# Three edits to a two-block network kernel: earlier split pieces in a narrow projection, a rotated key added once, chain products ahead of dense quarters

## The reference, cut to what matters

```python
# first network: output projection of the attention, a residual with a gate
h = h + gm * (jnp.concatenate([y_w, y_g, y_n], axis=-1) @ w_out[l])

# recurrent mix: inputs of its chunks, with decay products P
kk = kk / norm(kk);  k = k * (1 + (a - 1) * k_a)
bonus = sum(r * k * r_k) * v

# latent attention: one rotated key for all 8 heads
k_rope = _apply_rope(k_rope, cos, sin)
logits = (jnp.einsum('bhqd,bhkd->bhqk', q_nope, k_nope)
          + jnp.einsum('bhqd,bkd->bhqk', q_rope, k_rope))
```

## Time and profile before

| | |
|---|---|
| median of the runs | 2359.54 us |
| profiled execution, its own time | 2362.72 us |
| its span | 2361.4 us |
| mean granted TensorE clock | 0.984 |
| TensorE matmul busy | 2257.7 us, 96% |
| TensorE weight load busy | 1914.6 us, 81% |
| VectorE busy | 1501.5 us, 64% |
| ScalarE busy | 954.9 us, 40% |
| GpSimd busy | 367.7 us, 16% |

### The profile page before, as it was taken

How to read it: one execution, slowest core, us unless ns; L and a number is a source line. 1 busy time by engine, 2 the same in 40 slices (tenths; PEclk the granted TensorE clock), 3 DMA queues, 4 the chain that set the end, 5 groups by cost and what they waited for, 6 DMA issues and landing times. The chain is left out here.

```text
span 2361.4 us, 36947 instructions
## 1 busy us (share of the span) xinstructions
PE 2257.7 (96%) x14328; PEld 1914.6 (81%) x14328; DVE 1501.5 (64%) x2311; ACT 954.9 (40%) x1534; POOL 367.7 (16%) x365
## 2 busy tenths in 40 slices
PE   6999999999999999999999999979999999998998
PEld 4888887666678888878888876669998998898998
DVE  4666766565675666666565346556667766876874
ACT  4222223455442222242222244545446334555763
POOL 1000001000000000000000010039995476000000
PEclk9999999999999999999999999999999999999999
DMA  7554445111134444434443242124544232244544
GB/s 280 190 189 178 171 165 178 72 37 54 54 134 160 168 175 170 169 119 178 160 177 129 98 129 80 55 87 154 191 168 167 94 115 73 90 146 158 179 175 144
DMA packets 52615, 331.03 MB, mean 140 GB/s; under 512 B 6545, under 2 KB 7825, under 8 KB 21649
## 3 DMA queue, kind: packets, MB, share of 16 engines
q1 hardware_dynamic: 49040, 319.15, 37.4%
q0 software_dynamic: 3456, 10.25, 1.5%
HBM read 325.56 MB, written 3.80 MB: 139 GB/s over the span
## 5 line engine op out<-in xcount | busy, mean ns | idle before, releaser
L1183 PE MATMUL bank<-u_hi,whi 128*128 128x512 f32 (+1 forms) x2512 | 867.6, 345 | 32.5 <-DVE u_lo L1137 14.9
L1184 PE MATMUL bank<-u_lo,whi 128*128 128x512 f32 (+1 forms) x2512 | 848.7, 338 | 0.0
L1185 PE MATMUL bank<-u_hi,wlo 128*128 128x512 f32 (+1 forms) x2512 | 848.1, 338 | 0.0
L568 DVE TENSOR_TENSOR wlo<-raw,whi 128x2048 fp32r<-128x2048 f32 (+2 forms) x207 | 433.3, 2093 | 317.0 <-ACT whi L566 317.0
L1183 PEld LDWEIGHTS bank<-u_hi,whi 128*128 128x128 f32 x2512 | 477.2, 190 | 108.9 <-issue 29.5
L1185 PEld LDWEIGHTS bank<-u_hi,wlo 128*128 128x128 f32 x2512 | 477.5, 190 | 51.6
L1184 PEld LDWEIGHTS bank<-u_lo,whi 128*128 128x128 f32 x2512 | 477.8, 190 | 48.8 <-issue 0.2
L566 ACT ACTIVATE whi<-raw 128x2048 fp32r<-128x2048 f32 (+2 forms) x207 | 353.1, 1706 | 340.6 <-PE bank L1185 254.0
L1245 ACT ACTIVATE sil<-bank 128x512 f32<-128x512 f32 (+1 forms) x88 | 47.8, 544 | 541.7 <-PE bank L1185 541.7
L1183 PE MATMUL bank<-hidden_hi,whi 128*128 128x512 f32 x528 | 205.4, 389 | 0.0
L1184 PE MATMUL bank<-hidden_lo,whi 128*128 128x512 f32 x528 | 205.4, 389 | 0.0
(11 more groups left out here) (426 smaller groups left out, 2907.2 us busy)
## 6 DMA issues: line engine op xcount, KB each, us to landing
raw<-in_stream SPq DMA_DIRECT2D x231, 1024.0 KB, 4.8
raw<-in_stream SPq DMA_DIRECT2D x80, 704.0 KB, 4.0
first_ada<-in_stream SPq DMA_DIRECT2D x8, 1024.0 KB, 16.4
raw<-in_stream SPq DMA_DIRECT2D x8, 768.0 KB, 4.3
skew<-rpb_rows POOLq DMA_DIRECT2D x8, 336.0 KB, 6.2
nbr_bias<-skew POOLq DMA_DIRECT2D x24, 112.0 KB, 3.5
h<-in_tokens SPq DMA_DIRECT2D x1, 2048.0 KB, 11.5
uq_ukv<-in_small POOLq DMA_DIRECT2D x1, 1536.0 KB, 8.0
```

Source lines behind the costliest of these rows:

```text
L568: v.tensor_tensor(self.lo[to][:, 0:n], raw[:, 0:n], self.hi[to][:, 0:n].bitcast(F32), ALU.subtract).then_inc(self.s_lo, 1)
L1183: pe.q.matmul(dst, w[0], x[0], start=start, stop=False)
L1184: pe.q.matmul(dst, w[0], x[1], start=False, stop=False)
L1185: return pe.q.matmul(dst, w[1], x[0], start=False, stop=stop)
```

## The change

It makes three edits. In the narrow projection a tile emits two pieces of the split instead of one (the wide one stays). The rotated key is added into head 0 alone by VectorE, and ScalarE copies it to the 7 others; the scores of the latent attention wait for the copy. In the recurrent mix the three quarters of `dense(3)` are emitted behind the chain instead of ahead of it, together with the four that stood there.

```diff
--- before.py
+++ after.py
@@ -1655,6 +1655,8 @@
                         split_begin(*((PHASE[("out", l)], i // 4 + 1) if i < 12 else (PHASE[("up2", l)], 0)))
                 if k % step == step - 1:
                     split_next()
+                    if qn != T:
+                        split_next()
                     yield step * (0.69 if qn == T else 0.36)
             done = (st.s_pe, g + 1) if i % 4 == 3 else tile_done
 
@@ -2229,7 +2231,6 @@
     bb = dve.do(dve.q.tensor_tensor(aa[:, :, :], kk[:, :, :], aa[:, :, :], ALU.mult))
     dve.after(bb, grown)
     beta = dve.do(dve.q.tensor_tensor(aa[:, :, :], aa[:, :, :], dec[:, :, :], ALU.mult))
-    dense(3)
     dve.after(kp, faded, *[mixed[c] for c in range(4)])
     for c in range(4):
         t = dve.do(dve.q.scalar_tensor_tensor(out=bonus[:, c, :], in0=R[:, c, :], scalar=vcol("r_k", c),
@@ -2254,7 +2255,7 @@
 
     pool.after(kap)
     map_ready = rest_of_map(map_ready, (0, 1))
-    dense(4)
+    dense(7)
 
     def bank16(b0, c, k, hp, w=CH):
 
@@ -2703,8 +2704,7 @@
     def mla_inputs():
 
         dve.after(rwkv_out["done"], latent_done["turned"])
-        kr_done = dve.do(dve.q.tensor_tensor(
-            K2[rp, :, :], krr[rp, 0:1, :].to_broadcast([32, MH, S]), krr[rp, 1:2, :].to_broadcast([32, MH, S]), ALU.add))
+        kr_done = dve.do(dve.q.tensor_tensor(K2[rp, 0, :], krr[rp, 0, :], krr[rp, 1, :], ALU.add))
         pe.after(latent_done["latents"], sm_ready, rwkv_out["spread_read"])
         act.after(rwkv_out["done"])
         for t in range(2):
@@ -2713,6 +2713,8 @@
         act.after(z)
         for t in range(2):
             mla_ready["v"] = act.do(act.q.activation(vm[:, t, :], banks[2 + t][:, :], ACT.Copy))
+        act.after(kr_done)
+        mla_ready["turned"] = act.do(act.q.activation(K2[rp, 1:MH, :], K2[rp, 0:1, :].to_broadcast([32, MH - 1, S]), ACT.Copy))
         yield
         qfree = [mla_ready["v"], mla_ready["v"]]
         dve.after(kr_done)
@@ -2771,7 +2773,7 @@
 
     def mla_score(uu, m, bank):
         hh, qt = uu
-        pe.after(mla_ready[hh], mla_ready["v"])
+        pe.after(mla_ready[hh], mla_ready["v"], mla_ready["turned"])
         return pe.q.matmul(bank[:, 0:(qt + 1) * P], Q[0:96, hh, qt * P:(qt + 1) * P], K2[0:96, hh, 0:(qt + 1) * P],
                            start=True, stop=True)
```

## The result

The kernel with the three edits takes 2364.39 us (median of 12 runs, 2359.38 to 2368.21), the kernel before 2358.97 us beside it (12 runs, 2353.60 to 2361.83). The ratio is 1.0023, 95% interval 1.0014 to 1.0033: 5.4 us slower (3.3 to 7.8). The forecast was 2364.1 us, 0.2% slower.

What follows compares the result with a forecast made beforehand. TensorE was taken as the bound (busy 2257.7 of 2361.4 us), so VectorE or ScalarE work counts only where TensorE waits. Terms 1.4 + 2.0 + 1.2 + 0 = 4.6 us gave 2364.1 us, 0.2% slower; range 2354 to 2370.

Steps and rivals of the forecast that it cites:

- Part 1, the plain queue: Narrow projection, VectorE's queue: without stretched instructions the last h starts at 1589.1 us, 0.8 us earlier than before.
- Part 1, the stretch: Narrow projection: instructions lengthened beside GpSimd add 2.2 us, putting the last h at 1591.3 us, 1.4 us later.
- Part 2, the chain in front of wlo: Recurrent mix: the chain delays the whole-panel wlo; TensorE waits some 4.8 instead of 2.67 us, 2.0 us lost.
- Part 2, the clock: Behind that longer TensorE wait: granted clock falls (2 in 3), half clock for some 2.4 us, 1.2 us lost.
- Part 3: Second latent attention: VectorE gains 1.86 us, ScalarE's copy delays the same wlo; wait for the exponentials unchanged, 0 us.
- (a): Whole change: edits do what they look like, waits vanish and the chain costs nothing; -6.4 us, 2353.1 us; chance 0.18.
- (b): Whole change: forecast without a clock fall and with little stretching; 1.2 us slower, 2360.7 us; chance 0.17.
- (c): Both VectorE stages: GpSimd's additions stretch every wlo; 8.6 us slower, 2368.1 us; chance 0.13.

Runs made afterwards that it cites:

- e6: Two split pieces per tile in the narrow projection, without GpSimd's bias-map steps beside it (computes another result), against the kernel before: ratio 0.9991.
- e1: Only the two split pieces per tile in the narrow projection, against the kernel before: ratio 0.9997.
- e2: Only the chain of products ahead of the dense quarters, against the kernel before: ratio 1.0015, 3.5 us slower.
- e5: Kernel before without GpSimd's bias-map steps beside the narrow projection (computes another result), against the kernel before: ratio 0.9977.
- e10: Only the 4 bonus products of the chain ahead of the three dense quarters, against the kernel before: ratio 0.9994.
- e8: Kernel before with the raw-panel buffers in the other order from the differential input on, against the kernel before: ratio 0.9994.
- e3: Only the rotated key added once and copied by ScalarE ahead of the second half of whi, against the kernel before: ratio 0.9996.
- e9: Kernel before with the narrow projection's last wlo moved behind the last residual, against the kernel before: ratio 0.9996.
- e4: Rotated key added once, with ScalarE's copy behind the second half of whi, against the kernel before: ratio 0.9996.
- e7: Chain ahead of the dense quarters plus 16 filler matmuls on TensorE between the third and fourth quarter, against the kernel before: ratio 1.0028.
- e11: Last wlo behind the last residual, key copy behind whi's second half, and buffers in the other order, against the kernel before: 2355.52 us, ratio 0.9978.

## Why the prediction was right, and where its steps were not

The time (2364.1 against 2364.39 us) and the sign were right. The loss was 5.4 us (3.3 to 7.8) where 4.6 us were forecast; the times agree more closely because the kernel before took 2358.97 us beside it and not 2359.54, which is luck. The sum's three terms came out at 1.16 (1.4), 4.0 to 4.6 between executions in the same state (3.2) and 0.2 (0). Step by step:

- **Part 1, the plain queue.** Right: it said the last `h` at 1589.1 us without stretching, 37.25 us after tile 0; e6, without GpSimd, shows 37.24. The waits at tiles 6, 11, 14 and 15 are there, and none at tile 12.
- **Part 1, the stretch, was mis-sized.** 2.2 us were to remain in front of the last `h`; it was 0.88 us (38.12 - 37.24). But what the prediction had left out came behind it: from the last `h` to the next product e1 takes 7.00 us and before 5.92 (e6, without GpSimd, 5.47), since `wlo`, the norm's diagonal and `u_lo` meet GpSimd there. The two misses, -1.3 and +1.1 us, nearly cancel. The waits for `whi` were 0.40 and 0.53 us where 0.56 was taken; one of three vanished.
- **Part 2, the chain in front of wlo.** The place and the sign were right. The number of 2.0 us rests on a profile with a late DMA, and e2, with one too, bears it out: its `wlo` comes 2.2 us later (7.59 against 5.38 us). Between executions without one it is 3.3 us (7.59 against 4.29). The forecast wait of 4.8 us is the 4.87 of e2. In after it was 3.51, because without the earlier fall of the clock VectorE was 1.54 us ahead, while TensorE arrived at nearly the same time (20.7 us after `v_tokens`, 20.9 before).
- **Part 2, the clock.** It fell in both profiles with the chain ahead. 1.2 us were forecast; 1.3 (after) and 1.8 us (e2) were measured. The 2.4 us at half clock behind that forecast stood in no row; TensorE worked at the lower level for some 3.4 us in after and 4.4 us in e2.
- **Part 3.** Right in the sum (0 against 0.2 us; the copy took 1.69 us where 1.7 was taken). The idle stretch on VectorE was 2.00 us and not 0.8: `wlo` ran sooner and waited longer for the same `whi`.
- **Rivals.** (a) fell: nothing came earlier. (b) fell with the clock. (c), GpSimd stretching everything, fell by e5 and e6 in part 1: the stretching is there in both orders, and up to the last `h` the pieces pay less of it. In part 2 the `wlo` beside GpSimd took 2.28 us, as long as before (2.29).

What averages say of the whole: of seven profiles with the order and buffers of before here (e10 is not among them), three have the fall behind `v_tokens`, and the way to the transposes is 39.4 us on average. With the chain ahead and the same share of falls it would be 43.3 us (from 44.45 and 42.44). The difference of 3.9 us, plus 1.16 and 0.2, gives 5.3 us, against 5.4 measured. With so few profiles the frequency of the fall stays open, and so the close agreement is partly chance.

## What to carry to other kernels

Work moved ahead of a split on which TensorE waits costs its own length less the idle time VectorE had there, so read that idle time in more than one execution: here a fall of the clock 15 us earlier decided whether a DMA was late. Measure a local loss from an instruction of the limiting engine that lies ahead of every such difference; from `a*decay`, a VectorE instruction that moves with it, the buffers of e8 seemed to gain 1.6 us over e3 where they gain nothing. An edit that moves work from one engine to another gains only if the second engine's part does not stand ahead of the same product: the same key copy was worth nothing ahead of `whi` and 1.6 us behind it. Gains of 1.5 us that no ratio can show singly can be found by distances between the same two instructions, and added up until the times of the runs show them.

## What the runs showed of the hardware

The same products ran at two paces at the full granted clock. 128x256 matmuls of the split form, without any wait, from 2200 to 2240 us, first after, then e1_pieces (PE busy, count, PEclk):

```profile
2200.00:2220.00 20.00, 20.00 (x178) 1.00 0.50 175
2220.00:2240.00 20.00, 20.00 (x179) 1.00 0.54 202
```

```profile
2200.00:2220.00 20.00, 20.00 (x172) 1.00 0.56 199
2220.00:2240.00 20.00, 20.00 (x172) 1.00 0.47 169
```

The pace differs by 4%, 113 against 118 ns from start to start. It is no property of the kernel: before had the faster pace between 1625 and 1700 us, e2 from 1600 to 1675. In after's profile it gave some 4 us back behind 2150 us, which is much of why that execution was its fastest. What sets it is open.

A wait's length alone did not decide the clock. Ahead of the chunk products, after 2.66 and 2.67 us it stayed (e9, before), after 2.83 us it fell (e6), and TensorE then lost 2.7 us, more than behind the 4.87 us of e2 (1.8 us). At tile 12, after 2.58 to 2.60 us, it fell in before, e2, e4, e7 and e9 and stayed in e3, e8, e10 and e11. Behind the 0.41 to 0.43 us at `v_tokens` it fell in seven of 13 profiles. What a fall costs depends on who waits behind it: nothing at tile 12, where VectorE sets the pace, and 2.6 us at `v_tokens` (40.48 against 37.84 us), since it delays VectorE, then the DMA, then the split for which TensorE waits.
